# Last stage of a hybrid decoder layer: the residual sum made by DMA additions into the result

## The chip, the core and the metric

The kernel is one program on one core of a Trainium2 chip. Its time is the device time of one execution in microseconds (us), and the figure compared is the median of several runs. Six parts of the core matter here: TensorE (PE, matmuls), VectorE (DVE), ScalarE (ACT), GpSimd (POOL), SyncE (SP), and the 16 DMA engines that carry every transfer between the chip's memory (DRAM) and the on-chip SBUF. SP, ACT and POOL each issue DMAs from a queue of their own; in the profile q1 is the queue of SP's DMAs and q0 that of POOL's.

## What is computed

The layer is a token mixer followed by a mixture of experts, each with a normalisation, a gate and a residual sum. The end of the reference is what the change touches:

```python
    x = x + gt_m[:, None] * _rmsnorm(y, g_post_mix[layer])          # "the mixer's output", called x1 in the kernel
    h = _rmsnorm(x, g_pre_ffn[layer]) * (1.0 + sc_f[:, None]) + sh_f[:, None]
    y = _hier_moe(h.reshape(b * s, d), ...)                          # top-2 of 8 experts in one of 4 groups
    x = x + gt_f[:, None] * _rmsnorm(y, g_post_ffn[layer])           # the result
```

All arrays are float32. There are 2048 tokens of 1024 numbers, held as 16 tiles (TILES) of 128 rows, so that one tile is 512 KB. The result is 16 such tiles.

## The kernel before

The program runs in stages, each closed by a barrier of all engines: `normalise`, `project`, `attend`, `merge`, `mix_out`, `route`, `experts`, `combine`. Inside a stage each engine has a list of its own, written out by hand, and semaphores tie the lists together; no scheduler moves anything.

- `mix_out` computes the mixer's output tile by tile. ACT stores each tile to a DRAM tensor `x_mixed` (`x1_dram`), and the normalised and shifted `h` to `h_moe`.
- `experts` walks over some 48 blocks of 128 token rows. SP loads the weights of an expert in 12 parts (PARTS) into `raw_gu` and `raw_d`; ACT and DVE split each part into a high and a low half; PE multiplies. POOL gathers the rows of a block from `h_moe` by an indirect DMA (L1546) and adds the block's result into the DRAM tensor `y_sum` by an indirect DMA with addition (L1555). It waits for each addition to land before it goes on. After the last expert's weights have been split, SP loads the first 12 tiles of `x_mixed` into the 12 parts of `raw_gu` and `raw_d`, which are free by then (L1532 to L1537).
- `combine` makes the result. SP loads the 16 tiles of `y_sum` into `comb_y` (L1761), the gate row broadcast to 128 rows (L1764), and the last 4 tiles of `x_mixed` (LATE) into `comb_x` (L1768). ACT squares and sums tile t (L1781) and takes the root (L1783). DVE takes the reciprocal (L1800), scales the tile by it and by the gate (L1802, semaphore `scaled`), and adds the mixer's tile, which lies in `raw_gu`, `raw_d` or `comb_x` (L1795, semaphore `summed`). SP waits for `summed` and stores the tile to `out` (L1771), behind all of its own loads. POOL only sets one constant.

What sets the order in `combine` is SP's list (16 + 1 + 4 loads, then 16 stores, each store behind a wait) and DVE's list (reciprocal, scale, add, 16 times over).

Of the kernel before, what the change touches and what calls it, by code (L numbers as in the profile page):

```python
# [5 lines left out]
P = 128  # L6
D = 1024
SEQ = 2048
KD = D // P
TILES = SEQ // P  # L10
# [10 lines left out]
NE = EG * EPG  # L21
DE = 512
KE = DE // P
NB = 64
# [5 lines left out]
I32 = mybir.dt.int32  # L30
ALU = mybir.AluOpType
ACT = mybir.ActivationFunctionType
AX = mybir.AxisListType
ds = bass.ds
# [1189 lines left out]
GU, PARTS = 8, 12  # L1224


def x1_part(t, raw_gu, raw_d):
    return raw_gu[:, t, :, :, :].rearrange("p m k f -> p (m k f)") if t < GU else raw_d[:, t - GU, :]


def route(nc, logits, table, slot_rows, slot_place, slot_share, raw_gu, raw_d, w_gate, w_up, w_down):


# [212 lines left out]
                dve.wait_ge(rows_ready, 4)  # L1446


def experts(nc, table, slot_rows, slot_place, slot_share, ident, h_dram, raw_gu, raw_d, w_gate, w_up, w_down, y_sum, x1_dram):

# [2 lines left out]
    with ExitStack() as ctx:  # L1455
        s = Scope(nc, ctx, "moe")
# [19 lines left out]
        lo_taken = [s.sem(f"lo_taken{i}") for i in range(2)]  # L1476
        silu_ready = [s.sem(f"silu_ready{i}") for i in range(2)]
        hid_ready = [s.sem(f"hid_ready{i}") for i in range(2)]
        row_ready, row_seen, place_ready, turn_seen, added, scattered, y_ready, x1_loaded = (s.sem(n) for n in (
            "row_ready", "row_seen", "place_ready", "turn_seen", "added", "scattered", "y_ready", "x1_loaded"))  # L1480

        def entry(eng, r, b, top):
            return eng.value_load(table[0:1, r, ds(b, 1)], min_val=0, max_val=top)
# [31 lines left out]
        with nc.Block() as block:  # L1515
            @block.sync
            def _(sp):
                def load(e, before):

                    for g in range(PARTS):  # L1520
                        sp.wait_ge(lo_ready[g], before)
                        load_part(sp, g, e, raw_gu, raw_d, w_gate, w_up, w_down, part_loaded[g])

                for g in range(PARTS):
                    sp.sem_inc(part_loaded[g], 32 if g < GU else 16)  # L1525

                def reload(b):
                    with sp.If(entry(sp, 1, b, 1) > 0):
                        load(entry(sp, 0, b, NE - 1), entry(sp, 2, b, NE))

                by_twos(sp, lambda i: [reload(2 * i), reload(2 * i + 1)])

                cut = entry(sp, 2, NB, NE) + 1
                for g in range(PARTS):
                    sp.wait_ge(lo_ready[g], cut)
                    sp.dma_start(x1_part(g, raw_gu, raw_d), x1_dram[ds(g * P, P), :]).then_inc(x1_loaded, 16)
                sp.wait_ge(x1_loaded, 16 * PARTS)  # L1537

            @block.gpsimd
            def _(pool):  # L1540
# [194 lines left out]
                by_twos(dve, lambda i: [block_of(2 * i, 0), block_of(2 * i + 1, 1)])  # L1735


def combine(nc, y_sum, x1_dram, gate_dram, raw_gu, raw_d, out):

    LATE = TILES - PARTS  # L1740
    with ExitStack() as ctx:
        s = Scope(nc, ctx, "comb")
        y = s.sb("y", [P, TILES, D])
        x1 = s.sb("x1", [P, LATE, D])
        sq = s.sb("sq", [P, 2, D])
        mod = s.sb("mod", [P, D])
        eps = s.sb("eps", [P, 1])
        ms, root, rstd = s.sb("ms", [P, TILES]), s.sb("root", [P, TILES]), s.sb("rstd", [P, TILES])
        y_loaded = [s.sem(f"y_loaded{t}") for t in range(TILES)]
        x_loaded = [s.sem(f"x_loaded{t}") for t in range(LATE)]  # L1750
        mod_loaded, eps_ready, squared, rooted, recips, scaled, summed, stored = (s.sem(n) for n in (
            "mod_loaded", "eps_ready", "squared", "rooted", "recips", "scaled", "summed", "stored"))
        with nc.Block() as block:
            @block.gpsimd
            def _(pool):
                pool.memset(eps[:, :], EPS).then_inc(eps_ready, 1)

            @block.sync
            def _(sp):
                def load_y(t):  # L1760
                    sp.dma_start(y[:, t, :], y_sum[ds(t * P, P), :]).then_inc(y_loaded[t], 16)  # L1761

                load_y(0)
                sp.dma_start(mod[:, :], gate_dram.partition_broadcast(P)).then_inc(mod_loaded, 16)  # L1764
                for t in range(1, TILES):
                    load_y(t)
                for t in range(LATE):
                    sp.dma_start(x1[:, t, :], x1_dram[ds((PARTS + t) * P, P), :]).then_inc(x_loaded[t], 16)  # L1768
                for t in range(TILES):
                    sp.wait_ge(summed, t + 1)  # L1770
                    sp.dma_start(out[0, ds(t * P, P), :], y[:, t, :]).then_inc(stored, 16)  # L1771
                sp.wait_ge(stored, 16 * TILES)

            @block.scalar
            def _(act):
                act.wait_ge(eps_ready, 1)
                for t in range(TILES):
                    act.wait_ge(y_loaded[t], 16)  # L1778
                    if t >= 2:
                        act.wait_ge(squared, t - 1)  # L1780
                    nc.scalar.activation(sq[:, t % 2, :], y[:, t, :], ACT.Square, accum_out=ms[:, t:t + 1]).then_inc(squared, 1)  # L1781
                    act.wait_ge(squared, t + 1)
                    nc.scalar.activation(root[:, t:t + 1], ms[:, t:t + 1], ACT.Sqrt, scale=1.0 / D,  # L1783
                                         bias=eps[:, 0:1]).then_inc(rooted, 1)

            @block.vector
            def _(dve):
                def add(t):
                    dve.wait_ge(scaled, t + 1)
                    if t >= PARTS:  # L1790
                        dve.wait_ge(x_loaded[t - PARTS], 16)
                        mixed = x1[:, t - PARTS, :]
                    else:
                        mixed = x1_part(t, raw_gu, raw_d)
                    dve.tensor_tensor(y[:, t, :], y[:, t, :], mixed, ALU.add).then_inc(summed, 1)  # L1795

                dve.wait_ge(mod_loaded, 16)
                for t in range(TILES):
                    dve.wait_ge(rooted, t + 1)  # L1799
                    dve.reciprocal(rstd[:, t:t + 1], root[:, t:t + 1]).then_inc(recips, 1)  # L1800
                    dve.wait_ge(recips, t + 1)
                    dve.scalar_tensor_tensor(out=y[:, t, :], in0=y[:, t, :], scalar=rstd[:, t:t + 1],  # L1802
                                             in1=mod[:, :], op0=ALU.mult, op1=ALU.mult).then_inc(scaled, 1)
                    add(t)


def build(nc, x, c, w_ada, b_ada, g_pre_mix, g_post_mix, g_pre_ffn, g_post_ffn, w_in, w_pool_group, pool_scale,
          w_branch_pool, w_branch_att, w_out, w_group_router, b_group_router, w_expert_router, b_expert_router,
          w_exp_gate, w_exp_up, w_exp_down, out):
    def dram(name, shape, dt=F32):  # L1810
        return nc.dram_tensor(name, shape, dt).ap()
# [3 lines left out]
    proj = dram("projected", (IN_TILES * P, SEQ))  # L1815
    att = dram("attended", (len(DILATIONS), SEQ, HPG * ROW))
    merged = dram("merged", (D, SEQ))
    x1_dram = dram("x_mixed", (SEQ, D))
    h_dram = dram("h_moe", (SEQ, D))
    y_sum = dram("y_sum", (SUM_TILES * P, D))  # L1820
    with ExitStack() as ctx:
        def top(name, shape, dt=F32):
            return ctx.enter_context(nc.sbuf_tensor(name, shape, dt))

        ident = top("ident", [P, P])
        constants(nc, ident)
        with ExitStack() as mixer:
            h_hi = mixer.enter_context(nc.sbuf_tensor("h_hi", [P, KD, SEQ], F32R))
            h_lo = mixer.enter_context(nc.sbuf_tensor("h_lo", [P, KD, SEQ], F32R))
            act_c = mixer.enter_context(nc.sbuf_tensor("act_c", [P, KD], F32))  # L1830
            normalise(nc, x, c, w_ada, b_ada, g_pre_mix, ident, act_c, h_hi, h_lo)
            project(nc, w_in, w_ada, act_c, h_hi, h_lo, proj, ada_part, y_sum)
        attend(nc, proj, ident, att)
        merge(nc, proj, att, ident, w_pool_group, pool_scale, w_branch_pool, w_branch_att, merged)
        table, slot_rows = top("table", [1, 4, NB + 1], I32), top("slot_rows", [P, NB + 2], I32)
        slot_place, slot_share = top("slot_place", [P, NB], I32), top("slot_share", [P, NB])
        logits = top("logits", [P, TILES, NR])
        mix_out(nc, x, merged, w_out, ada_part, b_ada, (g_post_mix, g_pre_ffn, g_post_ffn), ident, w_group_router,
                w_expert_router, b_group_router, b_expert_router, gate_dram, x1_dram, h_dram, logits)
        raw_gu, raw_d = top("raw_gu", [P, GU, 2, 2, H2]), top("raw_d", [P, KE, D])  # L1840
        route(nc, logits, table, slot_rows, slot_place, slot_share, raw_gu, raw_d, w_exp_gate, w_exp_up, w_exp_down)
        experts(nc, table, slot_rows, slot_place, slot_share, ident, h_dram, raw_gu, raw_d, w_exp_gate, w_exp_up, w_exp_down,
                y_sum, x1_dram)
        combine(nc, y_sum, x1_dram, gate_dram, raw_gu, raw_d, out)


# [21 lines left out]
```

## Time and profile before

| What | Value |
|---|---|
| Median of 3 runs | 2713.99 us (2712.82 to 2718.81) |
| Profiled execution, its own time | 2717.12 us |
| Span of it, first to last instruction | 2715.4 us |
| PE busy | 2385.7 us (88%) |
| DVE busy | 1337.3 us (49%) |
| POOL busy | 534.0 us (20%) |
| DMA packets of q1 (SP's and others' hardware queue) | 424.53 MB, 45.1% of 16 engines |
| DMA packets of q0 (POOL's) | 51.39 MB, 8.0% of 16 engines |

Times inside the trace are counted from the start of the span. PE's last matmul ends shortly before 2645; the last addition into `y_sum` is issued at 2645.36, and `combine` starts at 2661.36 and ends with the span. In the section on rows, a row of a stretch gives the length, the busy time of each engine with its count of instructions, TensorE's granted clock, the busy share of the 16 DMA engines and what they moved in GB/s. A row of the time line gives start, length, engine, line, operation, output and inputs, and in square brackets the idle time ahead of it and what ended that. The busy time of a queue's packets can add up to a little over 100% of a stretch, since packets overlap on an engine.

### The profile page before, as it was taken

What the parts mean: (1) busy time and instruction counts of PE and PEld (TensorE: products, weight loads), DVE (VectorE), ACT (ScalarE), POOL (GpSimd) and SP (SyncE); (2) the same over time, 40 slices, a digit from 0 to 9 for tenths busy, and PEclk for the clock granted to TensorE, in tenths of its full rate; (3) what the DMA queues carried; (4) which work ended last, traced back from release to release, by engine and by line L of the source; (5) the groups of instructions that cost most, each with busy time, mean ns of one, the idle gap of its engine ahead of it and who ended that gap; (6) DMA issues with size and microseconds to landing.
All of it is one profiled execution on the core that took longest, in us unless ns stands there. A gap on an engine that the chain in (4) does not pass through costs nothing. (4 is left out here: it accounts for less than half of the span.)

```text
span 2715.4 us, 39222 instructions
## 1 busy us (share of the span) xinstructions
PE 2385.7 (88%) x13485; PEld 2043.5 (75%) x13486; DVE 1337.3 (49%) x1673; ACT 935.4 (34%) x1541; POOL 534.0 (20%) x375
## 2 busy tenths in 40 slices
PE   3599999999999977886977996599999999999990
PEld 3488888888888856783866885488889999999980
DVE  7553112123232257645533445888667385756536
ACT  3200000000000035533322221487666385656533
POOL 2311111111111020002334553121222122211220
PEclk9699999999999989957998997799999999999995
DMA  6123232323333233226646443499999598879847
GB/s 231 48 78 121 80 107 86 100 81 135 116 116 124 108 136 120 71 82 237 210 175 214 155 155 131 166 354 350 320 314 295 167 324 260 281 234 284 261 147 294
DMA packets 291435, 493.43 MB, mean 182 GB/s; under 512 B 21145, under 2 KB 226481, under 8 KB 281778
## 3 DMA queue, kind: packets, MB, share of 16 engines
q1 hardware_dynamic: 272658, 424.53, 45.1%
q0 software_dynamic: 14112, 51.39, 8.0%
q10 hardware_dynamic: 4608, 16.78, 1.6%
q8 instruction: 32, 0.52, 0.1%
q14 instruction: 25, 0.20, 0.0%
HBM read 374.98 MB, written 117.64 MB: 181 GB/s over the span
## 5 line engine op out<-in xcount | busy, mean ns | idle before, releaser
L357 PE MATMUL proj_psum<-h_hi,proj_w_hi 128*128 128x512 f32 x1216 | 481.8, 396 | 18.8 <-POOL proj_w_lo L342 18.8
L358 PE MATMUL proj_psum<-h_lo,proj_w_hi 128*128 128x512 f32 x1216 | 481.6, 396 | 0.0
L359 PE MATMUL proj_psum<-h_hi,proj_w_lo 128*128 128x512 f32 x1216 | 481.6, 396 | 0.0
L1585 PE MATMUL moe_p_gu<-moe_hi_gu,moe_xT_hi 128*128 128x256 f32 x1536 | 437.0, 285 | 1.7 <-DVE moe_xT_lo L1694 1.7
L378 DVE COPY proj_out<-proj_psum 128x512 f32<-128x512 f32 x152 | 123.6, 814 | 634.7 <-PE proj_psum L359 633.6
L1587 PE MATMUL moe_p_gu<-moe_hi_gu,moe_xT_lo 128*128 128x256 f32 x1536 | 428.4, 279 | 0.0
L1586 PE MATMUL moe_p_gu<-moe_lo_gu,moe_xT_hi 128*128 128x256 f32 x1536 | 428.4, 279 | 0.0
L1513 DVE TENSOR_TENSOR moe_lo_gu<-raw_gu,moe_hi_gu 128x1024 fp32r<-128x1024 f32 x256 | 302.5, 1221 | 28.2 <-ACT moe_hi_gu L1507 22.6
L335 ACT ACTIVATE proj_w_hi<-proj_raw 128x1024 fp32r<-128x1024 f32 x38 | 40.3, 1062 | 781.8 <-PE proj_psum L359 748.4
L1585 PEld LDWEIGHTS moe_p_gu<-moe_hi_gu,moe_xT_hi 128*128 128x128 f32 x1536 | 290.4, 189 | 4.2 <-issue 2.1
L1586 PEld LDWEIGHTS moe_p_gu<-moe_lo_gu,moe_xT_hi 128*128 128x128 f32 x1536 | 290.8, 189 | 2.2
L1587 PEld LDWEIGHTS moe_p_gu<-moe_hi_gu,moe_xT_lo 128*128 128x128 f32 x1536 | 290.7, 189 | 0.0
L357 PEld LDWEIGHTS proj_psum<-h_hi,proj_w_hi 128*128 128x128 f32 x1216 | 229.0, 188 | 74.6 <-issue 19.2
L359 PEld LDWEIGHTS proj_psum<-h_hi,proj_w_lo 128*128 128x128 f32 x1216 | 228.9, 188 | 55.5
L358 PEld LDWEIGHTS proj_psum<-h_lo,proj_w_hi 128*128 128x128 f32 x1216 | 228.9, 188 | 55.3
L1507 ACT ACTIVATE moe_hi_gu<-raw_gu 128x1024 fp32r<-128x1024 f32 x256 | 257.1, 1054 | 16.0 <-SPq L1525 11.3
L342 POOL TENSOR_TENSOR proj_w_lo<-proj_raw,proj_w_hi 128x1024 fp32r<-128x1024 f32 x38 | 97.8, 2574 | 725.0 <-ACT proj_w_hi L335 725.0
L1555 POOL DMA_INDIRECT y_sum<-moe_ys,moe_place x48 | 93.0, 1937 | 343.5 <-ACT moe_ys L1676 330.9
L1585 PE MATMUL moe_p_y<-moe_hi_d,moe_hT_hi 128*128 128x512 f32 x384 | 159.0, 414 | 0.3 <-DVE moe_hT_lo L1694 0.3
L1587 PE MATMUL moe_p_y<-moe_hi_d,moe_hT_lo 128*128 128x512 f32 x384 | 151.7, 395 | 0.0
L1586 PE MATMUL moe_p_y<-moe_lo_d,moe_hT_hi 128*128 128x512 f32 x384 | 151.7, 395 | 0.0
L1513 DVE TENSOR_TENSOR moe_lo_d<-raw_d,moe_hi_d 128x1024 fp32r<-128x1024 f32 x128 | 148.8, 1217 | 4.6 <-ACT moe_hi_d L1507 4.2
(268 smaller groups left out, 3660.9 us busy)
## 6 DMA issues: line engine op xcount, KB each, us to landing
raw_gu<-in_w_exp_gate SPq DMA_DIRECT2D x256, 256.0 KB, 5.8
raw_gu<-in_w_exp_up SPq DMA_DIRECT2D x256, 256.0 KB, 6.0
raw_d<-in_w_exp_down SPq DMA_DIRECT2D x128, 512.0 KB, 8.7
projected<-proj_out SPq DMA_DIRECT2D x38, 1024.0 KB, 3.9
proj_raw<-in_w_in SPq DMA_DIRECT2D x38, 512.0 KB
att_qkv<-projected SPq DMA_DIRECT2D x18, 1024.0 KB
proj_w_rest<-in_w_ada SPq DMA_DIRECT2D x8, 2048.0 KB
merge_gate<-projected SPq DMA_DIRECT2D x32, 512.0 KB, 4.9
```

Source lines behind the costliest of these rows:

```text
L335: nc.scalar.activation(w_hi[:, u, :, :], raw[:, u, :, :], ACT.Copy).then_inc(hi_ready[u], 1)
L342: pool.tensor_tensor(w_lo[:, u, :, :], raw[:, u, :, :], w_hi[:, u, :, :], ALU.subtract).then_inc(lo_ready[u], 1)
L357: pe.matmul(bank, w_hi[:, u, k, :], h_hi[:, k, tok], start=(k == 0), stop=False)
L358: pe.matmul(bank, w_hi[:, u, k, :], h_lo[:, k, tok], start=False, stop=False)
L359: mm = pe.matmul(bank, w_lo[:, u, k, :], h_hi[:, k, tok], start=False, stop=(k == KD - 1))
L378: ins = dve.tensor_copy(view[:, ds(tg * per, per), :], psum[:, u, tg, :].rearrange("p (m r) -> p m r", r=dilation))
L1507: nc.scalar.activation(hi_part(g), raw_part(g), ACT.Copy).then_inc(hi_ready[g], 1)
L1513: dve.tensor_tensor(lo_part(g), raw_part(g), hi_part(g), ALU.subtract).then_inc(lo_ready[g], 1)
L1555: pool.indirect_dma_start(out=y_sum, out_offset=bass.IndirectOffsetOnAxis(ap=place[:, u:u + 1], axis=0), in_=ys[:, u, :], in_offset=None, ...
L1585: pe.matmul(bank, x_hi, w_hi, start=first, stop=False)
L1586: pe.matmul(bank, x_hi, w_lo, start=False, stop=False)
L1587: return pe.matmul(bank, x_lo, w_hi, start=False, stop=last)
```

## The change

`mix_out` stores the mixer's tiles to `out` itself; the tensor `x_mixed` is gone. `experts` no longer loads any tile of it, and `combine` doesn't load the last four either. In `combine` DVE stops at the scaled tile. POOL builds a table of row numbers (`comb_place`, element (p, t) is 128 t + p) and then, for each tile, waits for `scaled` and issues an indirect DMA that adds the tile's 128 rows to the same rows of `out`. SP issues no store at all.

```diff
@@ experts, SP
-                cut = entry(sp, 2, NB, NE) + 1
-                for g in range(PARTS):
-                    sp.wait_ge(lo_ready[g], cut)
-                    sp.dma_start(x1_part(g, raw_gu, raw_d), x1_dram[ds(g * P, P), :]).then_inc(x1_loaded, 16)
-                sp.wait_ge(x1_loaded, 16 * PARTS)
@@ combine, POOL
                 pool.memset(eps[:, :], EPS).then_inc(eps_ready, 1)
+                pool.iota(place[:, :], pattern=[[P, TILES]], base=0, channel_multiplier=1).then_inc(place_ready, 1)
+                pool.wait_ge(place_ready, 1)
+                for t in range(TILES):
+                    pool.wait_ge(scaled, t + 1)
+                    pool.indirect_dma_start(out=out[0], out_offset=bass.IndirectOffsetOnAxis(ap=place[:, t:t + 1], axis=0),
+                                            in_=y[:, t, :], in_offset=None, compute_op=ALU.add).then_inc(added, 16)
+                pool.wait_ge(added, 16 * TILES)
@@ combine, SP
-                for t in range(LATE):
-                    sp.dma_start(x1[:, t, :], x1_dram[ds((PARTS + t) * P, P), :]).then_inc(x_loaded[t], 16)
-                for t in range(TILES):
-                    sp.wait_ge(summed, t + 1)
-                    sp.dma_start(out[0, ds(t * P, P), :], y[:, t, :]).then_inc(stored, 16)
-                sp.wait_ge(stored, 16 * TILES)
@@ combine, DVE
-                def add(t):
-                    dve.wait_ge(scaled, t + 1)
...
-                    dve.tensor_tensor(y[:, t, :], y[:, t, :], mixed, ALU.add).then_inc(summed, 1)
-
                 dve.wait_ge(mod_loaded, 16)
                 for t in range(TILES):
...
                                              in1=mod[:, :], op0=ALU.mult, op1=ALU.mult).then_inc(scaled, 1)
-                    add(t)
@@ build
         mix_out(nc, x, merged, w_out, ada_part, b_ada, (g_post_mix, g_pre_ffn, g_post_ffn), ident, w_group_router,
-                w_expert_router, b_group_router, b_expert_router, gate_dram, x1_dram, h_dram, logits)
+                w_expert_router, b_group_router, b_expert_router, gate_dram, out[0], h_dram, logits)
```

How the lists of instructions stand at the end of the program follows. First SP, from its last load in `experts` to its end; before:

```order
L1536 DMA raw_gu<-x_mixed 128x1024 x8
L1536 DMA raw_d<-x_mixed 128x1024 x4
L1515 UNCONDITIONAL_BRANCH
L1758 UNCONDITIONAL_BRANCH
L1761 DMA comb_y<-y_sum 128x1024
L1764 DMA comb_mod<-gate_ffn 128x1024
L1761 DMA comb_y<-y_sum 128x1024 x15
L1768 DMA comb_x<-x_mixed 128x1024 x4
L1771 DMA out<-comb_y 128x1024 x16
L1753 UNCONDITIONAL_BRANCH
```

and after, from the end of the same loop over the blocks:

```order
L1511 UNCONDITIONAL_BRANCH
L1754 UNCONDITIONAL_BRANCH
L1757 DMA comb_y<-y_sum 128x1024
L1760 DMA comb_mod<-gate_ffn 128x1024
L1757 DMA comb_y<-y_sum 128x1024 x15
L1742 UNCONDITIONAL_BRANCH
```

SP keeps its 17 loads and loses 16 loads of the mixer's tiles and 16 stores. Next POOL in `combine`, whose list before and after is

```order
L1754 UNCONDITIONAL_BRANCH
L1756 MEMSET comb_eps 128x1
L1753 UNCONDITIONAL_BRANCH
L72 ISA
```

```order
L1743 UNCONDITIONAL_BRANCH
L1745 MEMSET comb_eps 128x1
L1746 IOTA comb_place 128x16
L1750 DMA out<-comb_y,comb_place 2048x1024 x16
L1742 UNCONDITIONAL_BRANCH
L72 ISA
```

The 16 transfers of the result now stand on POOL's queue, behind one small table.

## Rows read from the trace of the kernel before

**Rows 1.** The page's chain that ended last: shares of the span, engine and line.

```profile
DVE comb_y L1802 1%; DVE comb_y L1795 1%; DMA comb_y<-y_sum 0%; DVE comb_rstd L1800 0%; ACT L1783 0%; ACT L1781 0%; ACT comb_sq L1781 0%; ACT comb_root L1783 0%; DVEq L1799 0%; ACTq L1778 0%
```

**Rows 2.** Time line of DVE in combine: first two tiles, last tile.

```profile
2669.40 1.28 DVE L1802 SCALAR_TENSOR_TENSOR comb_y<-comb_y,comb_rstd,comb_mod 128x1024 f32<-128x1024 f32 x1
2670.72 1.23 DVE L1795 TENSOR_TENSOR comb_y<-comb_y,raw_gu 128x1024 f32<-128x1024 f32 x1
2671.86 0.15 DVE L1800 RECIPROCAL comb_rstd<-comb_root 128x1 f32<-128x1 f32 x1
2672.05 1.28 DVE L1802 SCALAR_TENSOR_TENSOR comb_y<-comb_y,comb_rstd,comb_mod 128x1024 f32<-128x1024 f32 x1
...
2710.52 1.23 DVE L1795 TENSOR_TENSOR comb_y<-comb_y,comb_x 128x1024 f32<-128x1024 f32 x1
```

**Rows 3.** Time line of SP from 2560 on: its DMA issues.

```profile
2580.54 10.87 SPq L1536 DMA_DIRECT2D raw_gu<-x_mixed  x8
2592.23 3.73 SPq L1536 DMA_DIRECT2D raw_d<-x_mixed  x4
...
2677.23 34.87 SPq L1771 DMA_DIRECT2D out<-comb_y  x16
```

**Rows 4.** SP's last store, and the stores' landing times.

```profile
2711.77 0.33 SPq L1771 DMA_DIRECT2D out<-comb_y  x1
```

```profile
DMA to landing us min/median/max: 2.6/10.1/15.6
```

**Rows 5.** DMA of the stretch 2660 to 2716: q1's packets, MB, busy share.

```profile
q1 hardware_dynamic: 5328, 19.40, 87.4%
```

**Rows 6.** Stretches of combine, with DMA share and GB/s as last columns.

```profile
2663.00:2673.00 10.00, 0.00 (x0) 0.00 (x0) 3.69 (x5) 7.82 (x14) 0.00 (x0) 0.50 1.00 383
2673.00:2704.00 31.00, 0.00 (x0) 0.00 (x0) 30.16 (x37) 16.21 (x37) 0.00 (x0) 0.50 1.03 414
2704.00:2716.00 12.00, 0.00 (x0) 0.00 (x0) 7.57 (x8) 0.00 (x0) 0.00 (x0) 0.50 0.55 223
```

**Rows 7.** Stretches while SP loads the mixer's tiles in experts.

```profile
2580.00:2586.00 6.00, 6.00 (x43) 5.49 (x42) 4.82 (x7) 3.80 (x7) 3.06 (x3) 1.00 0.68 237
2592.00:2598.00 6.00, 6.00 (x55) 6.00 (x55) 5.23 (x7) 3.51 (x6) 2.22 (x1) 1.00 0.96 381
```

**Rows 8.** Time line of POOL in experts, with idle time ahead.

```profile
2594.86 2.22 POOL L1555 DMA_INDIRECT y_sum<-moe_ys,moe_place  x1 [10.58 <-ACT moe_ys L1676]
2604.68 0.18 POOL L1543 COPY moe_row<-slot_rows 128x1 int32 x1 [7.60 <-DMA y_sum<-moe_ys,moe_place]
2605.66 1.00 POOL L1546 DMA_INDIRECT moe_xg<-h_moe,moe_row  x1 [0.80 <-POOL moe_row L1543]
...
2645.36 1.60 POOL L1555 DMA_INDIRECT y_sum<-moe_ys,moe_place  x1 [8.90 <-ACT moe_ys L1676]
```

**Rows 9.** DMA of the stretch 2645 to 2653, one addition alone, 0.2 us slices.

```profile
DMA  0000000000009907179997998998100000000000
...
q0 software_dynamic: 144, 0.52, 41.6%
...
y_sum<-moe_ys,moe_place POOLq DMA_INDIRECT x1, 6.1
```

**Rows 10.** DMA of the stretch 2541.4 to 2549.7, one addition beside weight loads.

```profile
q1 hardware_dynamic: 898, 2.31, 72.3%
q0 software_dynamic: 144, 0.52, 31.7%
```

**Rows 11.** DMA of 1773.13 to 1782.16, an early addition beside weight loads.

```profile
q0 software_dynamic: 144, 0.52, 29.2%
```

**Rows 12.** DMA of 2648 to 2651.2: the lone addition without its first packets.

```profile
q0 software_dynamic: 128, 0.46, 76.1%
```

**Rows 13.** Time line of ACT in combine: the start of two following tiles.

```profile
2669.00 1.04 ACT L1781 ACTIVATE comb_sq<-comb_y 128x1024 f32<-128x1024 f32 x1
...
2670.37 1.04 ACT L1781 ACTIVATE comb_sq<-comb_y 128x1024 f32<-128x1024 f32 x1
```

More of the change, by code:

```diff
@@ L1224 @@
 GU, PARTS = 8, 12
-def x1_part(t, raw_gu, raw_d):
-    return raw_gu[:, t, :, :, :].rearrange("p m k f -> p (m k f)") if t < GU else raw_d[:, t - GU, :]
 def route(nc, logits, table, slot_rows, slot_place, slot_share, raw_gu, raw_d, w_gate, w_up, w_down):
@@ L1446, in _, with experts @@
                 dve.wait_ge(rows_ready, 4)
-def experts(nc, table, slot_rows, slot_place, slot_share, ident, h_dram, raw_gu, raw_d, w_gate, w_up, w_down, y_sum, x1_dram):
+def experts(nc, table, slot_rows, slot_place, slot_share, ident, h_dram, raw_gu, raw_d, w_gate, w_up, w_down, y_sum):
     with ExitStack() as ctx:
@@ L1478, in experts @@
         hid_ready = [s.sem(f"hid_ready{i}") for i in range(2)]
-        row_ready, row_seen, place_ready, turn_seen, added, scattered, y_ready, x1_loaded = (s.sem(n) for n in (
-            "row_ready", "row_seen", "place_ready", "turn_seen", "added", "scattered", "y_ready", "x1_loaded"))
+        row_ready, row_seen, place_ready, turn_seen, added, scattered, y_ready = (s.sem(n) for n in (
+            "row_ready", "row_seen", "place_ready", "turn_seen", "added", "scattered", "y_ready"))
         def entry(eng, r, b, top):
@@ L1735, in _, with combine @@
                 by_twos(dve, lambda i: [block_of(2 * i, 0), block_of(2 * i + 1, 1)])
-def combine(nc, y_sum, x1_dram, gate_dram, raw_gu, raw_d, out):
-    LATE = TILES - PARTS
+def combine(nc, y_sum, gate_dram, out):
     with ExitStack() as ctx:
@@ L1743, in combine @@
         y = s.sb("y", [P, TILES, D])
-        x1 = s.sb("x1", [P, LATE, D])
         sq = s.sb("sq", [P, 2, D])
@@ L1747, in combine @@
         eps = s.sb("eps", [P, 1])
+        place = s.sb("place", [P, TILES], I32)
         ms, root, rstd = s.sb("ms", [P, TILES]), s.sb("root", [P, TILES]), s.sb("rstd", [P, TILES])
         y_loaded = [s.sem(f"y_loaded{t}") for t in range(TILES)]
-        x_loaded = [s.sem(f"x_loaded{t}") for t in range(LATE)]
-        mod_loaded, eps_ready, squared, rooted, recips, scaled, summed, stored = (s.sem(n) for n in (
-            "mod_loaded", "eps_ready", "squared", "rooted", "recips", "scaled", "summed", "stored"))
+        mod_loaded, eps_ready, place_ready, squared, rooted, recips, scaled, added = (s.sem(n) for n in (
+            "mod_loaded", "eps_ready", "place_ready", "squared", "rooted", "recips", "scaled", "added"))
         with nc.Block() as block:
@@ L1787, in _ @@
             def _(dve):
-                def add(t):
-                    dve.wait_ge(scaled, t + 1)
[L1790 to L1794, printed above, removed]
-                    dve.tensor_tensor(y[:, t, :], y[:, t, :], mixed, ALU.add).then_inc(summed, 1)
                 dve.wait_ge(mod_loaded, 16)
@@ L1817, in build @@
     merged = dram("merged", (D, SEQ))
-    x1_dram = dram("x_mixed", (SEQ, D))
     h_dram = dram("h_moe", (SEQ, D))
@@ L1842, in build @@
         experts(nc, table, slot_rows, slot_place, slot_share, ident, h_dram, raw_gu, raw_d, w_exp_gate, w_exp_up, w_exp_down,
-                y_sum, x1_dram)
-        combine(nc, y_sum, x1_dram, gate_dram, raw_gu, raw_d, out)
+                y_sum)
+        combine(nc, y_sum, gate_dram, out)
 _INS = ["x", "c", "w_ada", "b_ada", "g_pre_mix", "g_post_mix", "g_pre_ffn", "g_post_ffn", "w_in", "w_pool_group",
```

## The prediction

> **What bounds the kernel now.** I read the chain of waits first, for the stage that ends the span: it is DVE's list in `combine`, scale and add in turn [rows 1]. The time line of DVE gives its rhythm: one scale starts at 2669.40, the next at 2672.05, so 2.65 us a tile, with hardly an idle moment until the last add starts at 2710.52 [rows 2]. The last store is issued at 2711.77 and takes 2.6 us to land [rows 4], at 2714.4; the span ends at 2715.4, 1.0 us later. The reader should then look past DVE. The stretches of `combine` show the DMA engines at a share of 1.00 and 1.03 and at 383 and 414 GB/s until 2704, and only then, with 0.55, not full [rows 6]. So this stage has two limits close together: DVE, and the DMA engines, which carry 37 tiles of 0.524 MB (16 of `y_sum`, the gate, 4 of the mixer, 16 stores). TensorE is idle in the stage, and nothing ahead of `combine` depends on what the change does there.
>
> **Prices of a transfer.** Here everything turns on what a DMA with addition costs the 16 engines. I count in packet time: the share of the 16 engines that a queue's packets took, times the stretch.
> - A plain tile: 87.4% of 56 us for 19.40 MB [rows 5] is 48.9 us for 37 tiles, 1.32 us each. At a share of 1.03 [rows 6] that is 1.28 us of wall time.
> - An addition beside weight loads: 31.7% of 8.3 us [rows 10] is 2.63 us. Another, 800 us earlier, gives 29.2% of 9.03 us [rows 11], 2.64 us. That is twice a plain tile for the same bytes moved.
> - An addition alone: 41.6% of 8 us [rows 9] is 3.33 us. The slices of that row show its engines busy from 2647.4 to 2650.8, first one packet each and then, after a gap, the other seven. Without the first packets there are 76.1% of 3.2 us [rows 12], 2.44 us for seven of eight packets, so 2.78 us for eight. In a row of additions that queue up the start is paid once.
> So an addition costs 2.63 to 2.78 us in a full queue and at most 3.33 us. I take 2.7. No row shows two additions queued behind one another, since `experts` waits for each; that is the largest unknown.
>
> **The change, part by part.**
> - Removed, the 12 loads of the mixer's tiles in `experts` (15.4 us of SP's time from 2580.54 to 2595.96 [rows 3]): worth nothing. PE is busy for 6.00 of 6.00 us while they run [rows 7], so TensorE hides them, and the addition that lands late beside them (issued at 2594.86, POOL goes on at 2604.68 [rows 8]) holds nobody that PE waits for. If PE had waited there, some us would be won; no row shows that it does.
> - `mix_out` stores to `out` in place of `x_mixed`: same issues, same bytes, zero.
> - Removed, DVE's 16 adds of 1.23 us [rows 2]. DVE's period falls from 2.65 us to about 1.39: the reciprocal starts 1.14 us into the add today, that is 0.09 before its end, so with the scale of 1.28 in its place it starts at 1.19 and the next scale 0.19 to 0.20 after that [rows 2]. ACT keeps 1.37 us a tile [rows 13], so it does not hold DVE while its loads are there. The first tile is scaled at 2670.7, as today, and the last at about 2691.5 in place of the last sum's 2711.75. This would be 20 us off the end if nothing else were late. The DMA engines are.
> - Removed, 4 loads of mixer tiles and 16 stores: 20 plain tiles, 26.4 us of packet time.
> - Added, 16 additions of 2.7 us: 43.2 us of packet time. The stage goes from 37 x 1.32 = 48.8 us to 17 x 1.32 + 43.2 = 65.6 us, and it was nearly full before.
> - Added, POOL's issues. One takes 1.60 us where DVE is idle and 2.22 us where DVE is busy (5.23 of 6 us) [rows 7, 8], and the row of the gather shows 0.80 us between the end of what it waits for and its start. So 3.02 us a tile while DVE works and 2.40 after it; without that gap 2.2 and 1.6. The first starts at 2670.7 + 0.8 = 2671.5, and the sixteenth at 2716.8 at the latest. Behind the waits of POOL nothing else is queued, and the one waiter for the additions is POOL at its end. The table of row numbers lies ahead of the first tile by over 8 us, so it is hidden by the loads.
>
> **The sum.** The loads run at full share from 2663 on [rows 6]; I start them at 2663.4, since the first us is still filling up. The first addition's data start 2.0 us behind its issue (2645.36, slices from 2647.4 [rows 8, 9]), at 2673.5. Until then, at 383 GB/s and a little more [rows 6], 4.0 MB of the 17 tiles' 8.9 are done. From there the queues share. Beside an addition q1 moved 2.31 MB in 8.3 us [rows 10], 278 GB/s; the remaining 4.9 MB so last 17.6 us, to about 2691.1, in which 17.6 / 8.3 = 2.1, say 2.3 additions get through. 13.7 additions are left, all queued or soon to be, at 2.7 us: 37.0 us, to 2728.1. From the last packet to the semaphore it takes 2645.36 + 6.1 - 2650.8 = 0.7 us [rows 8, 9], and 1.0 us more to the span's end: 2729.8, 14.4 us over 2715.4. With 2.63 it is 13.4, with 2.78 15.5. How the two queues share hardly matters, for the engines stay full either way: if they took packets in turn the loads would end later and the additions be further on. I take 15 us, 0.55%. The profiled execution took 2717.12 us against a median of 2713.99; I put the difference on the median: **2729 us**.
>
> **Rivals.**
> 1. Additions cost in a row what one costs alone, 3.33 us, because each packet waits for its read before its write: 13.7 x 3.33 = 45.6 us, end at 2738.4, +23, **2737 us**. For it: nothing else then fills the engines. Against: the seven later packets of rows 12 take less than the first.
> 2. **The other side:** additions cost as little as a store, and what looks like 2.63 us is packets that wait beside others. Then the engines have 33 plain tiles, 42.2 us of wall time, done at 2705.6, and POOL's issues decide. With the 0.80 us gap seven start up to 2689.6, the eighth at 2692.7, the last at 2711.9; with 6.1 us to landing [rows 9] and 1.0 behind it, 2719.0, +3.6, 2717.6 us: no change. Without the gap the ninth to tenth starts at 2691.5, the last at 2701.1, and the end is at 2708.2, -7.2, **2706.8 us**: faster. The point from which it decides is the price of an addition in wall time: 2663.4 + 17 x 1.28 + 16 c + 1.7 equals 2715.4 at c = 1.78 us. Against it: 3.33 us alone, with nothing beside it to wait for [rows 9].
> 3. POOL cannot issue while DVE scales. The rows show an issue lengthened from 1.60 to 2.22 us [rows 8], not stopped. If it were stopped until 2691.5, data would start at 2694.3, with the loads long done, and 16 x 2.7 = 43.2 us would end at 2737.5 + 1.7, +24, 2738 us.
> 4. The additions don't queue but follow one another at 6.1 us from issue to landing [rows 9]: 16 x 6.1 from 2671.5 is 2769, +54, 2768 us. Nothing in the code asks for it, and q0 is one queue.
>
> **The Trainium skill against the rows.** For rival 2: "DMA: Bandwidth & Descriptors", section "Anatomy of one DMA", fits a DMA from GpSimd as 2.0 us plus bytes over 436 GB/s. By it a further tile in a full queue would cost 1.2 us, an estimate from that page, addition or not. Rows 9 and 10 disagree with it for additions, by a factor of two and more. For rival 3: "SBUF — State Buffer", section "Who interferes with whom", says that a DVE instruction with two SBUF inputs (the scale is one) contends with a GpSimd instruction that reads SBUF, and that the later one fully blocks. Rows 8 show only 0.62 us of it.
>
> **How the numbers follow.** Forecast, +12 to +18 us: 0.57. Rival 1 and mixtures with it, to +27: 0.19. Rival 3: 0.05. Rival 2: 0.10, of which 0.04 faster and 0.06 no change. Rival 4 and other costs beyond: 0.09. The range, 2720 to 2742 us, leaves out rivals 2 and 4; its low end allows additions at 2.2 us, its high end 3.5. A measurement of this kernel can tell about 0.2%, 5.4 us, from no change: faster 0.04, same 0.06, slower 0.90.
>
> **What would show it.** Right: in the new profile DVE's last scale ends near 2692, the sixteen DMA_INDIRECT of `combine` start 2.2 to 3.1 us apart, the DMA share stays near 1 to the end while GB/s falls to about 200 once the loads are done, and POOL's last wait ends behind a DMA some 12 us or more after its last issue. The packet time of q0 in the stage divided by 16 gives the price directly. Wrong: a DMA share well under 1 between additions (POOL or latency decides), or 400 GB/s with additions alone (rival 2), or a PE with gaps in `experts` that are gone (I put those loads at zero).

## The result: 15 us slower, and the profile after

The changed kernel took 2729.64 us (median of 4 runs, 2726.09 to 2731.43) against 2714.86 us of the kernel before in the same runs, a ratio of 1.0045 with a 95% interval of 1.0028 to 1.0063. The forecast was 2729 us, with 2720 to 2742 as its range.

The profiled execution took 2731.43 us, with a span of 2729.6 us. Its last stage starts at 2662.43, where the one before started at 2661.36. The stage, from SP's first load to the end of the span, so lasts 67.2 us where it lasted 54.0: 13.1 us of the 14.2 between the two spans. This length is the figure to compare from here on. The start of the stage lies anywhere from 2654 to 2664 in the profiles of this case, for kernels that do the same up to there, so the total of one execution says little about a few us, and the medians below carry a few us of that too.

The page's chain of waits that ended last, which was DVE's list [rows 1], now goes through the loads. It only leads to POOL's last issue, which ends at 2708.73; the 20.9 us of the span behind that are in none of its entries, and are read from the DMA rows further down:

```profile
DMA comb_y<-y_sum 1%; SPq L1757 0%; POOL out L1750 0%; DVE comb_y L1783 0%; ACT comb_sq L1771 0%; SPq L1760 0%; ACT comb_root L1773 0%; DVE comb_rstd L1781 0%
```

The time line of DVE, to be laid beside [rows 2]: the scales follow one another at 1.39 us, later at 3.8 us, each behind an idle stretch that ACT ends.

```profile
2671.84 1.28 DVE L1783 SCALAR_TENSOR_TENSOR comb_y<-comb_y,comb_rstd,comb_mod 128x1024 f32<-128x1024 f32 x1
2673.04 0.16 DVE L1781 RECIPROCAL comb_rstd<-comb_root 128x1 f32<-128x1 f32 x1
2673.24 1.28 DVE L1783 SCALAR_TENSOR_TENSOR comb_y<-comb_y,comb_rstd,comb_mod 128x1024 f32<-128x1024 f32 x1
...
2701.63 0.16 DVE L1781 RECIPROCAL comb_rstd<-comb_root 128x1 f32<-128x1 f32 x1 [2.33 <-ACT comb_root L1773]
2701.83 1.28 DVE L1783 SCALAR_TENSOR_TENSOR comb_y<-comb_y,comb_rstd,comb_mod 128x1024 f32<-128x1024 f32 x1
2705.43 0.16 DVE L1781 RECIPROCAL comb_rstd<-comb_root 128x1 f32<-128x1 f32 x1 [2.31 <-ACT comb_root L1773]
```

ACT in turn waits for the loads of `y_sum`, 2.3 us each time (same kernel, time line of ACT):

```profile
2684.89 1.06 ACT L1771 ACTIVATE comb_sq<-comb_y 128x1024 f32<-128x1024 f32 x1 [2.34 <-DMA comb_y<-y_sum]
```

The time line of POOL, which had one constant to set:

```profile
2672.57 2.03 POOL L1750 DMA_INDIRECT out<-comb_y,comb_place  x1 [9.92 <-DVE comb_y L1783]
2674.90 2.43 POOL L1750 DMA_INDIRECT out<-comb_y,comb_place  x1 [0.30 <-issue]
2677.63 2.48 POOL L1750 DMA_INDIRECT out<-comb_y,comb_place  x1 [0.30 <-DVE comb_y L1783]
...
2687.84 1.54 POOL L1750 DMA_INDIRECT out<-comb_y,comb_place  x1 [0.31 <-issue]
...
2707.19 1.54 POOL L1750 DMA_INDIRECT out<-comb_y,comb_place  x1 [2.25 <-DVE comb_y L1783]
```

Stretches of the stage, columns as in [rows 6]:

```profile
2664.00:2674.00 10.00, 0.00 (x0) 0.00 (x0) 3.64 (x6) 7.77 (x14) 1.43 (x1) 0.50 0.98 382
2675.00:2705.00 30.00, 0.00 (x0) 0.00 (x0) 16.30 (x23) 15.65 (x35) 25.44 (x14) 0.50 1.06 284
2708.00:2726.00 18.00, 0.00 (x0) 0.00 (x0) 0.00 (x0) 0.00 (x0) 0.73 (x1) 0.50 1.07 211
```

The DMA engines are never short of work in these stretches (shares of 0.98, 1.06, 1.07), and the rate falls from 382 to 284 GB/s as soon as additions flow beside the loads, and to 211 when they are alone. After 2708.73 nothing but DMA is at work: the last addition lands 20 us behind its issue. The two queues over the whole stage, 2662.43 to 2729.6:

```profile
q0 software_dynamic: 2304, 8.39, 62.9%
q1 hardware_dynamic: 2448, 8.91, 35.3%
```

62.9% of 67.17 us is 42.2 us for 16 additions, 2.64 us each.

### The profile page after: what moved, and what is told of

Its sections match the earlier page's. It is cut to its first block and busy times, and to the rows that moved or that the text cites. A ratio compares the mean times of both kernels' runs of the same rounds, so it can differ in the third digit from the quotient of the medians.

```text
span 2729.6 us, 39183 instructions
## 1 busy us (share of the span) xinstructions
PE 2386.5 (87%) x13485; PEld 2041.7 (75%) x13486; DVE 1321.5 (48%) x1657; ACT 936.5 (34%) x1541; POOL 565.2 (21%) x392
## 5 line engine op out<-in xcount | busy, mean ns | idle before, releaser
L1503 ACT ACTIVATE moe_hi_gu<-raw_gu 128x1024 fp32r<-128x1024 f32 x256 | 257.3, 1054 | 17.2 <-SPq L1521 11.3
```

The source lines that it names most:

```text
L1503: nc.scalar.activation(hi_part(g), raw_part(g), ACT.Copy).then_inc(hi_ready[g], 1)
```

## The experiments

Each kernel was profiled once; those with a ratio were also timed, ten times each (e5 nine times), beside the kernel before. All lengths of the stage are read in the same way.

| Kernel | In the stage: plain tiles, additions | Stage, us | Ratio to before, 95% interval |
|---|---|---|---|
| before | 37, 0 | 54.0 | |
| changed | 17, 16 | 67.2 | 1.0045, 1.0028 to 1.0063 |
| e1_no_add | 33, 0 (16 of them by POOL) | 47.2 | 0.9971, 0.9955 to 0.9986 |
| e2_loads_back | 17, 16 | 67.2 | 1.0052, 1.0031 to 1.0073 |
| e3b_four_added | 29, 4 | 50.8 | 0.9973, 0.9955 to 0.9991 |
| e4_eight_added | 25, 8 | 55.9 | 1.0018, 0.9998 to 1.0039 |
| e5_adds_after_loads | 17, 16 | 73.0 | 1.0068, 1.0051 to 1.0084 |
| e6_dve_work_back | 17, 16 | 67.4 | 1.0054, 1.0033 to 1.0074 |
| e7_kept | 33, 0 | 54.1 | (one run) |
| e8_kept_pool4 | 33, 0 | 57.5 | 1.0009, 0.9992 to 1.0027 |
| e9_gate_psum_pool4 | 33, 0 | 52.2 | (one run) |
| e10_gate_psum_pool8 | 33, 0 | 51.2 | 0.9991, 0.9975 to 1.0006 |
| e11_gate_psum_pool10 | 33, 0 | 50.4 | 0.9984, 0.9969 to 0.9999 |

### Is it the addition, or POOL's path?

```diff
-                                            in_=y[:, t, :], in_offset=None, compute_op=ALU.add).then_inc(added, 16)
+                                            in_=y[:, t, :], in_offset=None).then_inc(added, 16)
```

> The changed kernel with the same sixteen indirect DMAs of POOL, but as plain writes without the addition, so that the mixer's part is missing from the result. Theory (the addition costs 2.64 us of packet time on the DMA engines, a plain tile 1.32): the engines have 33 tiles, about 42 us from 2664.5, done near 2707; POOL's issues then decide (2.75 us each while DVE is busy, 1.84 after), the last near 2708; span some 2713 us, 13 to 19 us under the changed kernel, about the kernel before or a little less. Packet time of q0 in the last stage about 1.3 us a tile. Rival (POOL's path and its row descriptors are what is dear, not the addition): within 4 us of the changed kernel.

Measured: 2710.05 us, a ratio to before of 0.9971; the stage is 47.2 us, 20.0 less than the changed kernel's. The queues over the stage, 2656.61 to 2703.8:

```profile
q1 hardware_dynamic: 2448, 8.91, 49.5%
q0 software_dynamic: 2304, 8.39, 43.4%
```

43.4% of 47.19 us is 20.5 us for 16 tiles, 1.28 us each: the same queue, the same rows, the same bytes at half the packet time. POOL's issues became shorter too, for the most part 1.07 to 1.09 us beside DVE and 0.96 without (time line of POOL):

```profile
2668.55 1.07 POOL L1750 DMA_INDIRECT out<-comb_y,comb_place  x1 [0.31 <-issue]
...
2686.42 0.96 POOL L1750 DMA_INDIRECT out<-comb_y,comb_place  x1 [1.53 <-DVE comb_y L1783]
```

So the addition is what costs. Why it costs double, and whether an addition without a list of rows would cost the same, these runs don't show. The stage lasted 47.2 us where I had worked out some 50.6: I had kept the addition's longer issues and let POOL decide, but its last issue started at 2693.93 and the engines were busy to about 2701, so the DMA engines ended this stage too. The kernel is no candidate, since it lacks the mixer's part; it shows what the stage would last if an addition cost as little as a write.

### Does the price hold for other counts?

With four additions, tiles 0, 3, 6 and 9 go POOL's way and the other twelve are summed by DVE from the parts loaded in `experts`; with eight, the even tiles go POOL's way.

```diff
+ADDED = [0, 3, 6, 9]
+SUMMED = [t for t in range(16) if t not in ADDED]
...
+                for t in ADDED:
+                    pool.wait_ge(scaled, t + 1)
+                    pool.indirect_dma_start(out=out[0], out_offset=bass.IndirectOffsetOnAxis(ap=place[:, t:t + 1], axis=0),
+                                            in_=y[:, t, :], in_offset=None, compute_op=ALU.add).then_inc(added, 16)
...
-                for t in range(TILES):
-                    sp.wait_ge(summed, t + 1)
+                for n, t in enumerate(SUMMED):
+                    sp.wait_ge(summed, n + 1)
...
-                    add(t)
+                    if t in SUMMED:
+                        add(t)
```

> The kernel before, with tiles 0, 3, 6 and 9 added by POOL's DMA and the other twelve summed by DVE from parts loaded in experts, so that combine loads no mixer tile; mix_out stores to the result. Packet time in the last stage 13 gate-and-load... in full: 17 loads and 12 stores of 1.32 us and 4 additions of 2.64 us, 48.8 us, as before (an addition costs what the load and the store that it replaces cost). Theory: DVE falls from 42.5 to about 37.5 us, the DMA engines decide at about 2711 to 2712, span 2711 to 2715, 0 to 3 us under the kernel before. Rival (an addition costs 3.3 us beside stores): 3 us over it.

> As with four added tiles, but the eight even tiles are added by POOL's DMA and the eight odd ones summed by DVE and stored by SP. Theory (1.32 us of packet time for a plain tile, 2.64 for an addition, engines full): 17 + 8 plain tiles and 8 additions, 54.1 us of packet time against 48.8 with four and 64.6 with sixteen, so the last stage, 50.8 us with four and 67.2 with sixteen, takes about 56 to 57 us: 2 to 3 us more than the 54.0 of the kernel before. Rival (the price lies in something paid once, as the start of POOL's queue): near 51 or near 67.

Measured: stages of 50.8 and 55.9 us. The queues with four additions (2654.99 to 2705.8), then with eight (2659.62 to 2715.5):

```profile
q1 hardware_dynamic: 4176, 15.21, 76.5%
q0 software_dynamic: 576, 2.10, 20.7%
```

```profile
q1 hardware_dynamic: 3600, 13.11, 61.3%
q0 software_dynamic: 1152, 4.19, 37.7%
```

20.7% of 50.81 us over 4 and 37.7% of 55.88 us over 8 are 2.63 us each, as against 2.64 with sixteen: in these three kernels the price depends neither on how many there are nor on how many loads and stores run beside them. From eight to sixteen the stage grows by 11.3 us, 1.41 us for each addition that takes the place of a store, where 2.64 - 1.32 gives 1.32. With four, both limits are reached: DVE is busy for 31.16 of 32 us, and the DMA engines stand at a share of 1.04:

```profile
2668.00:2700.00 32.00, 0.00 (x0) 0.00 (x0) 31.16 (x38) 15.19 (x34) 7.59 (x3) 0.50 1.04 350
```

At the end it is the DMA engines that are late:

```profile
2699.00 1.23 DVE L1799 TENSOR_TENSOR comb_y<-comb_y,raw_d 128x1024 f32<-128x1024 f32 x1
2700.25 0.33 SPq L1779 DMA_DIRECT2D out<-comb_y  x1
```

DVE's last sum ends 45.2 us into the stage, 5.1 us sooner than before (50.4), but the last store now takes 4.6 us to land, behind others, where it took 2.6, and the stage is only 3.2 us shorter.

This is the valid version with the lowest time: 2711.47 us, ratio 0.9973. It holds because four additions cost the engines about what the loads and stores cost that they replace (packet time of the stage 49.4 us against 48.9 before), so four tiles can leave DVE almost free of charge; the fifth would replace a store alone.

### Does the order of loads and additions matter?

```diff
+                for t in range(TILES):
+                    pool.wait_ge(y_loaded[t], 16)
                 for t in range(TILES):
                     pool.wait_ge(scaled, t + 1)
```

> The changed kernel, but POOL waits for the last of the 16 loads before its first addition. Theory (only the sum of the packet time counts, not how the queues share): the loads end near 2686, 16 additions in a row at 2.6 to 2.7 us from about 2689 end near 2732, span 2 to 5 us over the changed kernel, and q0's packet time stays 2.6 to 2.8 us a tile with nothing beside it. Rival (additions alone cost 3.33 us each): 14 us over it. Rival (sharing itself cost something): faster than the changed kernel.

Measured: 2735.48 us, ratio 1.0068 against 1.0052 of e2_loads_back, which was timed beside it and behaves as the changed kernel; the stage is 73.0 us, 5.8 more. Here 14 additions stand in a row with nothing beside them (DMA of 2690 to 2726):

```profile
DMA packets 2052, 7.49 MB, mean 208 GB/s; under 512 B 223, under 2 KB 223, under 8 KB 2052
...
q0 software_dynamic: 2052, 7.49, 106.3%
```

7.49 MB are 14.3 tiles in 36 us: 2.52 us of wall time and 2.68 us of packet time each. The rival of 3.33 us is out, and so is the one by which sharing costs something. I had expected 2 to 5 us. For 3.3 of the 5.8 us, from 2682.7 to 2686.0, between the last load and the first addition's data, no packet moves at all, and the first addition's packets then start thinly, as those of a lone one do [rows 9]; the remainder I did not take apart.

### Were the other parts worth anything?

The 12 loads in `experts` put back, their data unused:

```diff
+                for g in range(PARTS):
+                    sp.wait_ge(lo_ready[g], cut)
+                    sp.dma_start(x1_part(g, raw_gu, raw_d), x1_dram[ds(g * P, P), :]).then_inc(x1_loaded, 16)
```

> The changed kernel with the 12 loads of the mixer's tiles put back into experts (their data are not used). Theory (those loads are hidden by TensorE): the same as the changed kernel within 3 us, about 2729 us. Rival (their removal bought some us that the additions then lost): 3 to 10 us slower than the changed kernel.

Measured: 2729.16 us; the timing can tell about 0.2%, some 5 us. The stage (67.18 us against 67.17) says nothing here, since these loads lie ahead of it. What does is the time from one addition into `y_sum` ahead of the loads to the last one. In the changed kernel, then with the loads back:

```profile
2540.38 2.21 POOL L1546 DMA_INDIRECT y_sum<-moe_ys,moe_place  x1 [11.61 <-ACT moe_ys L1667]
2646.33 1.60 POOL L1546 DMA_INDIRECT y_sum<-moe_ys,moe_place  x1 [9.21 <-ACT moe_ys L1667]
```

```profile
2535.52 2.21 POOL L1556 DMA_INDIRECT y_sum<-moe_ys,moe_place  x1 [11.61 <-ACT moe_ys L1677]
2641.39 1.60 POOL L1556 DMA_INDIRECT y_sum<-moe_ys,moe_place  x1 [9.37 <-ACT moe_ys L1677]
```

That is 105.95 us without the loads and 105.87 with them (105.89 in the kernel before): they cost nothing, to 0.1 us. PE is as full beside them as in [rows 7]:

```profile
2588.00:2594.00 6.00, 6.00 (x56) 6.00 (x55) 5.26 (x7) 3.53 (x6) 2.22 (x1) 1.00 1.01 379
```

DVE's sixteen sums given back as work that nobody reads:

```diff
+                    dve.wait_ge(scaled, t + 1)
+                    if t >= 2:
+                        dve.wait_ge(spared, t - 1)
+                    dve.tensor_tensor(spare[:, t % 2, :], y[:, t, :], mod[:, :], ALU.add).then_inc(spared, 1)
```

> The changed kernel with DVE's sixteen additions of 1.23 us given back to it as work whose result nobody reads, behind each scaled tile. Theory (DVE is not what ends the changed stage): the stage stays at 67 us within 1 us, the whole within 3 us of the changed kernel. Rival (the shorter DVE work was worth something, or busy DVE holds up POOL's issues enough to starve the DMA engines): 3 us or more longer.

Measured: 2730.58 us, stage 67.4 us. Fourteen of POOL's sixteen issues now take 2.35 us, where most took 1.54, and it makes no difference:

```profile
2703.14 2.35 POOL L1752 DMA_INDIRECT out<-comb_y,comb_place  x1 [0.30 <-DVE comb_y L1785]
```

The 20 us that DVE saves are worth nothing in the changed kernel. POOL's last issue starts 49.3 us into the stage in place of 44.8, and those 4.5 us cost nothing either.

### What bounded the kernel before, and can it be relieved without additions?

The last four mixer tiles also loaded during `experts`, into a tensor of their own; `combine` then carries 33 tiles:

```diff
+                for t in range(PARTS, TILES):
+                    sp.dma_start(x1_late[:, t - PARTS, :], x1_dram[ds(t * P, P), :]).then_inc(x1_loaded, 16)
...
-                for t in range(LATE):
-                    sp.dma_start(x1[:, t, :], x1_dram[ds((PARTS + t) * P, P), :]).then_inc(x_loaded[t], 16)
```

> The kernel before, with the last four mixer tiles also loaded during experts, into a place of their own, so that combine carries 33 tiles in place of 37. Theory (DVE ends the stage of the kernel before, at 2.65 us a tile): stage 54 us within 0.5, no gain. Rival (the DMA engines are the bound there): 5 us less.

Measured: stage 54.05 us against 54.04. Four tiles less are worth nothing, so DVE alone set the end of the kernel before. Then four of the sums moved to GpSimd's own ALU:

```diff
+    ON_POOL = [2, 6, 10, 13]
...
+                for t in ON_POOL:
+                    pool.wait_ge(scaled, t + 1)
+                    pool.tensor_tensor(y[:, t, :], y[:, t, :], x1_part(t, raw_gu, raw_d, x1_late), ALU.add).then_inc(done[t], 1)
...
-                    add(t)
+                    if t not in ON_POOL:
+                        add(t)
```

> The same with all 16 mixer tiles in SBUF, and the sums of tiles 2, 6, 10 and 13 made by GpSimd's own ALU in place of DVE. If GpSimd's 2.6 us of a sum run beside DVE undisturbed: DVE ends 5 us earlier, DMA engines at 42 us of work, stage about 49 us, whole 5 us under the kernel before. If DVE and GpSimd block each other: 4 sums of 2.6 us come on DVE's path in place of 4 of 1.26, stage 59 us or more.

Measured: stage 57.5 us, 3.4 more. The time lines of POOL and DVE show why: a scale that starts just behind GpSimd's sum takes 3.41 us in place of 1.28 and ends 1.09 us after the sum, so nearly all of it ran behind the sum. All four are alike (3.39 to 3.41): 8.5 us more on DVE's list, where the four sums taken off it are 4.9.

```profile
2676.43 2.35 POOL L1762 TENSOR_TENSOR comb_y<-comb_y,raw_gu 128x1024 f32<-128x1024 f32 x1 [14.61 <-DVE comb_y L1801]
```

```profile
2676.46 3.41 DVE L1801 SCALAR_TENSOR_TENSOR comb_y<-comb_y,comb_rstd,comb_mod 128x1024 f32<-128x1024 f32 x1
```

This agrees with the rule of the Trainium skill ("SBUF — State Buffer", section "Who interferes with whom") that a DVE instruction with two SBUF inputs contends with a GpSimd instruction that reads SBUF. In these runs GpSimd always comes first and DVE waits; none shows the other way round. So the gate row was copied to PSUM once, and the scale left with one SBUF input:

```diff
+                dve.tensor_copy(mod_p[:, :, :].rearrange("p a c -> p (a c)"), mod[:, :]).then_inc(mod_moved, 1)
+                dve.wait_ge(mod_moved, 1)
...
-                                             in1=mod[:, :], op0=ALU.mult, op1=ALU.mult).then_inc(scaled, 1)
+                                             in1=mod_p[:, :, :].rearrange("p a c -> p (a c)"), op0=ALU.mult, op1=ALU.mult).then_inc(scaled, 1)
```

> As with all mixer tiles kept and four sums on GpSimd, but the gate row is copied once into PSUM, so that DVE's scale has only one input in SBUF. In the run without this copy each of the four scales beside a GpSimd sum took 3.40 us in place of 1.28, and the stage 57.5 us. Theory (the two engines block each other only where DVE reads two SBUF inputs): the scales stay near 1.3 us, DVE's sums may wait for GpSimd up to 1 us each, stage 49 to 53 us. Rival (any DVE instruction beside GpSimd's sum is blocked): stage 57 us again.

> The same with the eight even tiles summed by GpSimd (2.35 us each) and the eight odd ones by DVE. DVE alone would take 16 x 1.39 + 8 x 1.26 = 32.3 us, GpSimd 19; where DVE's sum meets a GpSimd sum it waits about 1 us, 8 us in all: 40 us, stage about 51 us, whole 2 to 4 us under the kernel before. If the waits are smaller, the DMA engines' 33 tiles decide: stage 48 us, 6 us under it. If GpSimd blocks the scales too: 57 us or more.

> The same with ten tiles summed by GpSimd (two of three, and two of the last four), six by DVE. DVE alone 16 x 1.39 + 6 x 1.26 = 29.8 us, GpSimd 24; with 1 to 2 us of waiting for each of DVE's six sums 36 to 42 us. Stage 47 to 51 us, whole 3 to 7 us under the kernel before.

Measured: stages of 52.2, 51.2 and 50.4 us. In the first of them the scale beside GpSimd's sum is back at 1.28 us; DVE's own sum behind it, with both inputs in SBUF, takes 2.10 in place of 1.23 and again ends 1.09 us after GpSimd's:

```profile
2678.26 2.35 POOL L1764 TENSOR_TENSOR comb_y<-comb_y,raw_gu 128x1024 f32<-128x1024 f32 x1 [14.37 <-DVE comb_y L1805]
```

```profile
2678.28 1.28 DVE L1805 SCALAR_TENSOR_TENSOR comb_y<-comb_y,comb_rstd,comb_mod_p 128x1024 f32<-128x1024 f32 x1
2679.60 2.10 DVE L1796 TENSOR_TENSOR comb_y<-comb_y,raw_gu 128x1024 f32<-128x1024 f32 x1
```

With ten sums on GpSimd, four of DVE's six sums find two GpSimd sums ahead of them and take 3.00 to 3.04 us, 1.8 more than alone, which eats most of what the split brings. The last version's gain, 0.16% with an interval that ends at 0.9999, is just measurable; four additions by DMA do about as much (stage 50.8 us against 50.4) with less. That e9 to e11, with less on DVE's list and the same transfers as e7_kept, end sooner than it also fits DVE as the limit there.

## Why the prediction was right, point by point

- **The bound.** I saw two limits close together. Both are confirmed: without four loads nothing is won (e7_kept), so DVE alone ended the stage; and with DVE 5.1 us shorter and the DMA work about the same, only 3.2 us are won (e3b_four_added), since the DMA engines then end it.
- **How near the number came.** Partly luck. The sum gave 14.4 us, 15 were taken, and the medians differ by 14.8; but the stage, which is what the sum describes, grew by 13.1. In the two profiled executions 1.1 us more lies in where the stage starts; what the medians have beyond that I did not take apart. Inside the stage two errors offset each other. The last packet was forecast 66.7 us into the stage (2728.1, counted from 2661.36) and came at 64.3 (2726.7, from 2662.43): for nearly the same packet time, the engines ran at shares of 1.06 and 1.07. From there to the end of the span I took 1.7 us, and it was 2.9:

```profile
DMA  9494949595959492110000000000000000000000
```

  These are slices of 0.15 us of the changed kernel from 2724 on; the last addition lands 0.6 us behind its last packet, and 2.3 us more pass to the end of the span, where I took 1.0 from a store of SP's. In all runs whose stage ends with POOL's transfers (also e1, e5 and e6) the whole tail is 2.7 to 3.1 us, in those that end with SP's stores (before, e3b, e4, e7) 1.3 to 1.5. What fills it, no row shows.
- **The price of an addition**, the term that carries the sum: 2.63 to 2.78 us of packet time, 2.7 taken. Measured 2.64 in the changed kernel, 2.63 with four and with eight, 2.68 in a row. Three things were a little off. In a full queue packets overlap (shares of 1.06 and 1.07), so that the wall time of one is 2.48 us alone (3.80 MB in 18 us) or 2.52 (e5), not 2.7. The plain tiles beside them cost 1.39 us of packet time each (35.3% of 67.17 us over 17), not 1.32. And the 3.33 us of rival 1 belonged to a lone addition's start, as the row of fourteen in e5 shows.
- **The stage's packet time**: forecast 65.6 us, measured (62.9% + 35.3%) of 67.17 us, 66.0; additions 1.0 us less than forecast, plain tiles 1.3 us more.
- **How the queues share.** Wrong, and harmless. I took 278 GB/s for the loads beside an addition, and the loads' end at 2691.1; measured is the stretch 2676 to 2703:

```profile
q0 software_dynamic: 947, 3.49, 64.6%
q1 hardware_dynamic: 1157, 4.19, 41.1%
```

  that is 155 GB/s for the loads and 129 for the additions, nearly half and half, and the last load is there only at about 2703.9. The step that failed is the reading of [rows 10]: in the stretch of 8.3 us the addition moved data for only some 3 us, as the slices of that same stretch show, where 18 slices stand at 336 GB/s or more before the first low one:

```profile
GB/s 390 395 400 415 395 395 474 336 454 434 355 434 395 434 395 395 454 336 158 375 197 336 237 276 217 336 237 276 296 257 257 197 360 148 370 331 380 370 385 370
```

  The mean over a stretch wider than the overlap is not the rate in the overlap. The middle of that stretch alone (kernel before, 2545.3 to 2548.4) would have said 126 GB/s for the loads:

```profile
q0 software_dynamic: 111, 0.45, 71.9%
q1 hardware_dynamic: 116, 0.39, 33.6%
```

  For the same reason DVE's last scale ends at 2706.9, not near 2692 as I had listed among the signs. It cost nothing, because the additions still to be done kept the engines full, as the sum had argued.
- **When additions start to move data.** I took 2.0 us behind the issue, from a lone one. In the changed kernel the rate falls only at about 2678, 5.4 us behind the first issue at 2672.57, and POOL's queue has no packet at all from 2674 to 2677.5; the engines work on loads until then. Harmless for the same reason.
- **POOL's issues.** Bounded at 2.2 to 3.02 us beside DVE and 1.6 to 2.40 after. Measured: 2.03 for the first, 2.43 to 2.48 while DVE scales without a pause, and 1.54 to 1.67 later. The 0.80 us that I set behind every wait was there only once: the first issue starts 0.84 us after the scale that it waits for, all others 0.3 us after the scale or the issue ahead of them. So they start 2.33 to 2.79 us apart at first and then 1.84 to 1.97, below the 2.2 that I had listed among the signs, with 2.37 and 3.80 before the last two, whose tiles come late. The last starts 44.8 us into the stage, and the engines have 19 us of backlog by then.
- **Rivals 3 and 4** are out. Five issues ran while DVE scaled, longer but not stopped (2.03 to 2.48 us), and the additions did queue: the last lands 20.1 us behind its issue, and at the end one takes 2.5 us, not 6.1.
- **Zero for the loads in `experts`, zero for DVE's saving**: confirmed, the first by e2_loads_back to 0.1 us over the last 106 us of `experts`, the second by e6_dve_work_back to 0.2 us of the stage.
- **The break-even of 1.78 us an addition.** e1_no_add gives the side below it: at 1.28 us of packet time the stage is 6.9 us shorter than before, beside the 7.2 worked out for rival 2 without the gap. That they agree is partly chance: rival 2 had POOL's last issue decide, and in e1_no_add the DMA engines did, busy to 44.5 us into the stage (rival 2 had them done at 44.2), with the longer tail of POOL's transfers behind. The break-even itself no run meets.

## What to carry to other kernels

Ask of a DMA that adds what else it does: here it took twice the packet time of a plain transfer of the same bytes, so it is about free where it replaces a load and a store, and dear where it replaces a store alone or where the other operand was loaded under cover. When a stage has two limits a few per cent apart, moving work off one of them only shows the other; measure each by taking work from it alone, as e7_kept did here. A rate beside another queue has to be read in the slices in which both move data.

## What the runs showed of the hardware that I had not expected

- An indirect DMA with addition takes GpSimd longer to issue, too: 1.54 us against 0.96 for the same rows without it, and 2.48 against 1.09 while DVE scales without a pause.
- Beside full engines, the first addition's data came 5.4 us behind its issue, 2.0 when alone, and then POOL's and SP's queues moved 129 and 155 GB/s. In which proportion the engines share in general, these runs don't tell.
- GpSimd's sum of two SBUF tiles, 2.35 us for 128 x 1024, held back a DVE instruction with two SBUF inputs that started behind it until it was over (3.41 us in place of 1.28), and one with an SBUF and a PSUM input not at all (1.28).
- A stage that ends with POOL's DMAs has 2.7 to 3.1 us from its last packet to the end of the span, one that ends with SP's stores 1.3 to 1.5.
